# Merging the low-rank and the preparation stage of the RWKV-7 mixer, with the key products spread over other engines

## The reference, cut to what matters

```python
r, k, v = jnp.einsum('pbtd,pde->pbte', xs[:3], w_rkv)
w = -jax.nn.softplus(-(w0 + jnp.tanh(xw @ w1) @ w2)) - 0.5
a = jax.nn.sigmoid(a0 + (xa @ a1) @ a2)
g = jax.nn.sigmoid(xg @ g1) @ g2
kk = heads(k * k_k)
kk = kk / jnp.maximum(jnp.sqrt(jnp.sum(kk * kk, -1, keepdims=True)), 1e-12)
k = k * (1 + (a - 1) * k_a)
decay = jnp.exp(-jnp.exp(heads(w)))
# the scan then takes r, decay, k, v, -kk and kk * a, and
# sum(r * k * r_k) over a head weighs v in a bonus term
```

## Time and profile before

| what | value |
|---|---|
| median of three runs | 1500.87 us |
| the profiled execution | 1502.7 us |
| its span | 1501.0 us |
| mean granted TensorE clock | 0.968 of full |
| TensorE busy (matmul) | 1407.5 us, 94% |
| VectorE busy | 853.3 us, 57% |
| ScalarE busy | 679.3 us, 45% |
| GpSimd busy | 233.0 us, 16% |

### The profile page before, as it was taken

How to read it: one execution, slowest core, us unless ns; L and a number is a source line. 1 busy time by engine, 2 the same in 40 slices (tenths; PEclk the granted TensorE clock), 3 DMA queues, 4 the chain that set the end, 5 groups by cost and what they waited for, 6 DMA issues and landing times. The chain is left out here.

```text
span 1501.0 us, 18775 instructions
## 1 busy us (share of the span) xinstructions
PE 1407.5 (94%) x7494; PEld 1135.2 (76%) x7494; DVE 853.3 (57%) x1158; ACT 679.3 (45%) x992; POOL 233.0 (16%) x127
## 2 busy tenths in 40 slices
PE   6999899989999989889999998998999998999998
PEld 2685467967888877467788886887887788977887
DVE  0764685467555454546755446566545677645564
ACT  1442343136444353344643334654563657426562
POOL 0003443004000022120400000120001332500110
PEclk7899799989999999799999999999999999999999
DMA  9655457074656556635566535952542453007940
GB/s 343 206 196 160 166 200 278 1 245 122 211 180 210 180 183 204 229 112 168 169 192 200 184 137 148 198 177 83 184 162 74 156 173 107 29 29 193 226 143 29
DMA packets 159395, 247.17 MB, mean 165 GB/s; under 512 B 14086, under 2 KB 98026, under 8 KB 158796
## 3 DMA queue, kind: packets, MB, share of 16 engines
q1 hardware_dynamic: 157980, 239.60, 50.8%
q0 software_dynamic: 1328, 6.38, 1.2%
HBM read 244.85 MB, written 4.24 MB: 166 GB/s over the span
## 5 line engine op out<-in xcount | busy, mean ns | idle before, releaser
L199 DVE TENSOR_TENSOR w_lo<-w_raw,w_hi 128x2048 fp32r<-128x2048 f32 (+3 forms) x176 | 411.7, 2348 | 293.5 <-ACT w_hi L190 293.4
L211 PE MATMUL ps<-w_hi,act_hi 128*128 128x512 f32 (+4 forms) x1216 | 471.3, 388 | 13.3 <-DVE w_lo L199 4.7
L213 PE MATMUL ps<-w_hi,act_lo 128*128 128x512 f32 (+4 forms) x1216 | 461.9, 380 | 0.0
L212 PE MATMUL ps<-w_lo,act_hi 128*128 128x512 f32 (+4 forms) x1216 | 461.5, 380 | 0.0
L190 ACT CAST w_hi<-w_raw 128x2048 fp32r<-128x2048 f32 (+3 forms) x176 | 316.9, 1806 | 254.6 <-PE ps L213 209.8
L211 PEld LDWEIGHTS ps<-w_hi,act_hi 128*128 128x128 f32 x1216 | 229.9, 189 | 60.2 <-issue 14.8
L213 PEld LDWEIGHTS ps<-w_hi,act_lo 128*128 128x128 f32 x1216 | 229.5, 189 | 38.4
L212 PEld LDWEIGHTS ps<-w_lo,act_hi 128*128 128x128 f32 x1216 | 230.1, 189 | 34.5 <-issue 0.5
L320 PE MATMUL ps<-w_raw,condz 128*32 128x512 f32 x384 | 63.3, 766 | 18.7 <-DMA w_raw<-in_ada_w 14.7
L672 POOL TENSOR_TENSOR nstat<-nstat,con 128x1 f32<-128x1 f32 x8 | 5.4, 678 | 429.4 <-DVE nstat L667 429.4
L211 PE MATMUL ps<-w_hi,ffn_gh 128*128 128x512 f32 x176 | 69.1, 393 | 0.0
(11 more groups left out here) (489 smaller groups left out, 1798.2 us busy)
## 6 DMA issues: line engine op xcount, KB each, us to landing
w_raw<-in_ada_w SPq DMA_DIRECT2D x48, 1024.0 KB, 6.8
w_raw<-in_ffn_w_in SPq DMA_DIRECT2D x88, 512.0 KB, 4.8
w_raw<-in_fox_w_in SPq DMA_DIRECT2D x32, 912.0 KB, 8.7
w_raw<-in_ffn_w_out SPq DMA_DIRECT2D x20, 1024.0 KB, 5.0
w_raw<-in_rwkv_w_rkv SPq DMA_DIRECT2D x12, 1024.0 KB, 6.3
w_raw<-in_gla_w_in SPq DMA_DIRECT2D x10, 896.0 KB, 4.9
w_raw<-in_gdn_w_in SPq DMA_DIRECT2D x10, 896.0 KB, 4.9
w_raw<-in_fox_w_out SPq DMA_DIRECT2D x8, 1024.0 KB, 5.1
```

What stands on the lines that cost most here:

```text
L199: self.nc.vector.tensor_tensor(lo[:, s, 0:c["nk"], 0:c["width"]], self.raw[:, c["slot"], 0:c["nk"], 0:c["width"]], hi[:, s, 0:c["nk"], 0:c ...
L211: nc.tensor.matmul(out(t)[:, 0:w], xh[:, k, tok], hi[:, s, j, 0:w], start=start, stop=False)
L212: nc.tensor.matmul(out(t)[:, 0:w], xh[:, k, tok], lo[:, s, j, 0:w], start=False, stop=False)
L213: return nc.tensor.matmul(out(t)[:, 0:w], xl[:, k, tok], hi[:, s, j, 0:w], start=False, stop=stop)
```

## The change

`stage_rwkv_lora` and `stage_rwkv_prepare` become one stage, `stage_rwkv_low`. The product of k with `k_k`, its squares, their sums and the limit from below go to VectorE in `stage_rwkv_in`, behind the last two chunks, as do the two input mixes for `w1` and `g1`; the rows `k_k` and `k_a` are loaded there. In the new stage the down products of `a1` and `w1` alternate and write different halves of the partitions in two banks; the last 32 columns of `g1` come later, behind the cumulative sums; the gate's up products come after the sums across tiles. The scale of the rates moves into the exponentials. VectorE's work on k and GpSimd's product of a and kk go tile by tile. The bonus sums go to the start of the next stage. The new stage has three modulation items where the two old ones had four, and `stage_rwkv_mid` has ten where it had nine.

The diff, cut (the bodies of the two removed functions and the placing of buffers are left out):

```diff
...
-def stage_rwkv_in(core, m, h, dx, xs, low_w):
+def stage_rwkv_in(core, m, h, dx, xs, low_w, key):
     nc, a, ps = core.nc, core.a, core.ps
     w1, a1, g1 = low_w
+    kk, st, k_a = key
+    k_k = core.gates
...
         @block.sync
         def _(sp):
@@ -1343,8 +1349,11 @@
             sp.dma_start(g1[:, :, :], a["rwkv_g1"][0].rearrange("(k p) n -> p k n", p=P)).then_inc(sem("low_w"), 16)
             core.issue(sp, chunks[len(chunks) // 2]["g"])
             sp.dma_start(core.con[:, 2 * P:], a["consts"][:, 2 * P:]).then_inc(core.consts, 16)
+            sp.dma_start(k_k[:, :], a["rwkv_k_k"].broadcast_to([P, D])).then_inc(sem("k_k"), 16)
+            sp.dma_start(k_a[:, :], a["rwkv_k_a"].broadcast_to([P, D])).then_inc(sem("k_a"), 16)
             core.issue(sp, chunks[-1]["g"] + 1 + NRAW)
             sp.wait_ge(sem("low_w"), 48)
+            sp.wait_ge(sem("k_a"), 16)
             sp.wait_ge(core.consts, 16)
         @block.tensor
...
-            steps(lambda c: core.split_lo(dve, hi, lo, c), lambda n: None, operand, mixed)
+            def keys(n):
+                if n == 2 * per + 2:
+                    dve.wait_ge(sem("k_k"), 16)
+                    dve.wait_ge(sem("taken"), 4 * NT)
+                    nc.vector.tensor_tensor(kk[:, :, :], m.k[:, :, :], bc_out(k_k[:, :], NT), ALU.mult).then_inc(sem("kk"), 1)
+                if n == 2 * per + 3:
+                    dve.wait_ge(sem("kk"), 1)
+                    nc.vector.tensor_tensor(flat(m.lw), flat(kk), flat(kk), ALU.mult).then_inc(sem("kk"), 1)
+                    dve.wait_ge(sem("kk"), 2)
+                    nc.vector.reduce_sum(st[:, 0:32], by_head(m.lw), axis=AX_X).then_inc(sem("kk"), 1)
+                    dve.wait_ge(sem("kk"), 3)
+                    nc.vector.tensor_scalar(st[:, 32:64], st[:, 0:32], 1e-24, None, ALU.max).then_inc(sem("kk"), 1)
+            steps(lambda c: core.split_lo(dve, hi, lo, c), lambda n: None, operand, mixed, keys)
             mixed(3)
...
+            mix(core, dve, sem, 3, dx, h, decay_in)
+            mix(core, dve, sem, 5, dx, h, gate_in)
+def stage_rwkv_low(core, m, w, xs, low_w, key, at, free, items):
+    nc, a, ps = core.nc, core.a, core.ps
+    kn, st, k_a = key
+    kk, rk = w["kk"], w["rk"]
...
+    ada = Ada(core, w["ada_at"], items, 3, 2)
+    with core.stage("rwkv_low") as (block, sem):
+        @block.sync
+        def _(sp):
+            sp.dma_start(w2[0:64, :], a["rwkv_w2"][0]).then_inc(sem("w2"), 16)
+            sp.dma_start(w2[64:65, :], a["rwkv_w0"]).then_inc(sem("w2"), 16)
+            sp.dma_start(a2[0:64, :], a["rwkv_a2"][0]).then_inc(sem("a2"), 16)
+            sp.dma_start(a2[64:65, :], a["rwkv_a0"]).then_inc(sem("a2"), 16)
+            sp.dma_start(g2[:, 0, :], a["rwkv_g2"][0, 0:P]).then_inc(sem("g2"), 16)
+            sp.dma_start(g2[0:32, 1, :], a["rwkv_g2"][0, P:160]).then_inc(sem("g2"), 16)
+            sp.dma_start(w["rows"][:, 2, :], a["rwkv_r_k"].rearrange("a h j -> a (h j)").broadcast_to([P, D])).then_inc(sem("r_k"), 16)
+            core.issue_mod(sp, items)
+            sp.wait_ge(sem("r_k"), 16)
+        @block.tensor
+        def _(pe):
+            def up(u, parts):
+                if u >= 4:
+                    pe.wait_ge(sem("up_out"), u - 3)
+                c = u % 2 * COLS
+                for n, (x, down) in enumerate(parts):
+                    r = nc.tensor.matmul(ps[:, 4 + u % 4, :], x, down[:, c:c + COLS], start=(n == 0), stop=(n == len(parts) - 1))
+                r.then_inc(sem("up"), 1)
+            def cum(t):
+                for i, tri in enumerate(("cum_in", "cum_ex")):
+                    for c in range(2):
+                        r = nc.tensor.matmul(ps[:, 4 * t + 2 * i + c, :], core.c(tri), m.lw[:, t, c * COLS:c * COLS + COLS],
+                                             start=True, stop=True)
+                    r.then_inc(sem("cum"), 1)
+            for k in range(KD):
+                nc.tensor.matmul(ps[0:64, 0, 0:T], a1[:, k, :], xs[:, k, :], start=(k == 0), stop=(k == KD - 1))
+                r = nc.tensor.matmul(ps[64:P, 1, 0:T], w1[:, k, :], decay_in[:, k, :], start=(k == 0), stop=(k == KD - 1))
+            r.then_inc(sem("down"), 1)
+            for k in range(KD):
+                r = nc.tensor.matmul(ps[:, 2, 0:T], g1[:, k, 0:P], gate_in[:, k, :], start=(k == 0), stop=(k == KD - 1))
+            r.then_inc(sem("down"), 1)
+            pe.wait_ge(sem("ones"), 1)
+            pe.wait_ge(sem("low"), 2)
+            for i, (x, n) in enumerate(((w2, "w2"), (a2, "a2"))):
+                pe.wait_ge(sem(n), 32)
+                for t in range(NT):
+                    for c in range(2):
+                        up(4 * i + 2 * t + c, [(low[0:65, i, 0, t * P:t * P + P], x[0:65, :])])
+            pe.wait_ge(sem("low"), 3)
+            pe.wait_ge(sem("up_out"), 4)
+            cum(0)
+            pe.wait_ge(sem("up_out"), 8)
+            cum(1)
+            pe.wait_ge(sem("exps"), 2)
+            for k in range(KD):
+                r = nc.tensor.matmul(ps[0:32, 0, 0:T], g1[:, k, P:160], gate_in[:, k, :], start=(k == 0), stop=(k == KD - 1))
+            r.then_inc(sem("down"), 1)
+            pe.wait_ge(sem("exps"), 3)
+            for k in range(KD):
+                nc.tensor.matmul(ps[:, 1, k:k + 1], m.lw[:, 0, k * P:k * P + P], core.c("half1"), start=True, stop=False)
+                r = nc.tensor.matmul(ps[:, 1, k:k + 1], m.lw[:, 1, k * P:k * P + P], core.c("half0"), start=False, stop=True)
+            r.then_inc(sem("across"), 1)
+            ada.pe_sums(pe, sem, 0)
+            pe.wait_ge(sem("g2"), 32)
+            pe.wait_ge(sem("low"), 4)
+            pe.wait_ge(sem("exps"), 6)
+            for t in range(NT):
+                tok = slice(t * P, t * P + P)
+                for c in range(2):
+                    up(8 + 2 * t + c, [(low[:, 2, 0, tok], g2[:, 0, :]), (low[0:32, 2, 1, tok], g2[0:32, 1, :])])
+            ada.pe_turn(pe, sem, 0)
+            for n in range(1, len(items)):
+                ada.pe_sums(pe, sem, n)
+                ada.pe_turn(pe, sem, n)
+        @block.scalar
+        def _(act):
+            act.wait_ge(sem("down"), 1)
+            nc.scalar.activation(low[0:64, 0, 0, :], ps[64:P, 1, 0:T], ACT.Tanh).then_inc(sem("low"), 1)
+            nc.scalar.copy(low[0:64, 1, 0, :], ps[0:64, 0, 0:T]).then_inc(sem("low"), 1)
+            act.wait_ge(sem("down"), 2)
+            nc.scalar.activation(low[:, 2, 0, :], ps[:, 2, 0:T], ACT.Sigmoid).then_inc(sem("low"), 1)
+            for u in range(8):
+                i, t, c = u // 4, u // 2 % 2, u % 2
+                act.wait_ge(sem("up"), u + 1)
+                nc.scalar.activation((m.lw, m.a)[i][:, t, c * COLS:c * COLS + COLS], ps[:, 4 + u % 4, :], ACT.Sigmoid).then_inc(sem("up_out"), 1)
+            for t in range(NT):
+                act.wait_ge(sem("cum"), 2 * t + 2)
+                c_in = ps[:, 4 * t:4 * t + 2, :].rearrange("p a b -> p (a b)")
+                c_ex = ps[:, 4 * t + 2:4 * t + 4, :].rearrange("p a b -> p (a b)")
+                nc.scalar.activation(ep[:, t, :], c_in, ACT.Exp, scale=-shrink).then_inc(sem("exps"), 1)
+                nc.scalar.activation(en[:, t, :], c_in, ACT.Exp, scale=shrink).then_inc(sem("exps"), 1)
+                nc.scalar.activation(ex[:, t, :], c_ex, ACT.Exp, scale=-shrink).then_inc(sem("exps"), 1)
+            act.wait_ge(sem("across"), 1)
+            nc.scalar.activation(w["across"][:, :], ps[:, 1, 0:KD], ACT.Exp, scale=-shrink).then_inc(sem("across_e"), 1)
+            act.wait_ge(sem("down"), 3)
+            nc.scalar.activation(low[0:32, 2, 1, :], ps[0:32, 0, 0:T], ACT.Sigmoid).then_inc(sem("low"), 1)
+            ada.act_part(act, sem, 0)
+            for u in range(8, 12):
+                t, c = u // 2 % 2, u % 2
+                act.wait_ge(sem("up"), u + 1)
+                nc.scalar.copy(m.g[:, t, c * COLS:c * COLS + COLS], ps[:, 4 + u % 4, :]).then_inc(sem("up_out"), 1)
+            for n in range(1, len(items)):
+                ada.act_part(act, sem, n)
+        @block.gpsimd
+        def _(pool):
+            nc.gpsimd.tensor_tensor(st[:, 32:64], st[:, 32:64], core.c("mhalf")[:, 0:32], ALU.pow).then_inc(sem("rn"), 1)
+            pool.wait_ge(sem("kn"), 1)
+            for t in range(NT):
+                pool.wait_ge(sem("up_out"), 6 + 2 * t)
+                pool.wait_ge(sem("less"), t + 1)
+                nc.gpsimd.tensor_tensor(A[:, t, :], A[:, t, :], kn[:, t, :], ALU.mult).then_inc(sem("kka"), 1)
+        @block.vector
+        def _(dve):
+            link = Link(dve, sem("dve"))
+            v = nc.vector
+            v.memset(low[64:65, 0:2, 0, :], 1.0).then_inc(sem("ones"), 1)
+            dve.wait_ge(sem("rn"), 1)
+            v.tensor_tensor(by_head(kn), by_head(kn), bc_in(st[:, 32:64], 64), ALU.mult).then_inc(sem("kn"), 1)
+            dve.wait_ge(sem("kn"), 1)
+            for t in range(NT):
+                dve.wait_ge(sem("up_out"), 6 + 2 * t)
```

(30 more changed lines are left out.)

148 lines of the change are left out of this document (16 added, 132 removed).

## The result

The changed kernel takes 1507.38 us (median of 13 runs, 1499.02 to 1518.56), the kernel before beside it 1503.3 (13 runs, 1496.52 to 1508.19): **ratio 1.0039, 95% interval 1.0022 to 1.0057**, some 3 to 9 us slower. The forecast was 1502.8 and "no difference". The measured median lies inside the range of 1495 to 1509, but a small loss clear of noise was measured where none was forecast. The 1502.8 was reckoned from 1500.87, the median of three runs; 13 runs of the kernel before have 1503.3, so 2.4 of the 4.6 us between forecast and median are the starting value. As a change, +1.9 us was forecast, and +4.1 by the medians or +5.9 by the ratio was measured. The profiled execution took 1506.51 us, its span is 1504.8.

What follows compares the result with a forecast made beforehand. TensorE's queue was taken to bound the two merged stages, 36.3 and 21.5 of 1501 us. Merged stage −2.3, mid's start −1.4 and mid's end +5.6 sum to +1.9 us: 1502.8 on the median, range 1495 to 1509.

Steps and rivals of the forecast that it cites:

- sign of being wrong: Mid's tail: the prediction is wrong if it grows by less than 3 or more than 8 us.
- End of mid: Mid's tail: the tenth item goes where nothing covers it and its chunks land late, +5.6 us (ends +3.0 and +7.7).
- outer end: Mid's tail: turns at the lower clock, 1.87 us each instead of 1.0, making the tail +7.7 us.
- End of the input stage: Input stage: with its added work VectorE ends it at 122.1 instead of ScalarE at 119.74, +2.35 us.
- Down products: Merged stage: a1 and w1 overlap in alternate column halves, 3.65 us for the pair; −4.1 us together, −0.45 without overlap.
- Gate's up products: Merged stage: following one-column products, they run 4 us at half clock, +2.0 us (ends 0 and +4).
- Table loads: Merged stage, ScalarE: two loads of 1.28 us, the second done before TensorE asks; costs nothing.
- Items and the wait for chunk 5: Merged stage's end: TensorE waits from 169.7 to 171.3 for a late-issued chunk, then half an item at lower clock.
- Start of mid: Mid's start: the small rel_bias load arrives 5.1 us after the start instead of 6.5, −1.4 us (ends −2.2 and 0).
- bunched items: Slower rival: no chunk issued for 29 us in the merged stage, price at both tails; +8.7 us, 1509.6, chance 0.13.

Runs made afterwards that it cites:

- Experiment 1: Kernel before with only one modulation item moved from the preparation stage to mid (ten there): 1505.86 us, ratio 1.0019.
- experiment 4: Changed kernel plus four useless 512-column products on TensorE behind the recurrence, to keep the tail's clock up: 1506.24 us, ratio 1.0030.
- experiment 9: Changed kernel with all down products of a1 ahead of those of w1 instead of in turn: 1511.41 us, ratio 1.0063.
- experiment 3: Changed kernel with the input mix for g1 back in the merged stage, under the down products of a1 and w1: 1503.93 us, ratio 1.0013.
- experiment 10: Changed kernel with the product of a and the normalized keys on VectorE instead of GpSimd: 1509.63 us, ratio 1.0036.
- experiment 6: Changed kernel with eight items in mid's loop instead of seven, one fewer in the tail: 1501.48 us, ratio 0.9986.
- experiment 5: Changed kernel with the merged stage's first item early, behind the down products: 1509.0 us, ratio 1.0040.
- experiment 7: Changed kernel with gate mix back in the merged stage, first item early and eight items in mid's loop: 1502.93 us, ratio 0.9984.
- Experiment 12: Changed kernel with gate mix back, four items spread through the merged stage, seven in mid's loop, two in its tail: 1494.05 us, ratio 0.9932.
- experiment 2: Changed kernel with the item's move undone, four items in the merged stage and nine in mid: 1502.87 us, ratio 1.0000.
- experiment 8: Changed kernel with gate mix back, four items spread through the merged stage, nine in mid, eight of them in its loop: 1494.33 us, ratio 0.9938.

## Why the prediction was wrong

The sum was +1.9 us; the profile says +5.24. The tail grew by more than the 8 us that the prediction had named as a sign of being wrong. Term by term the account is off by −0.3 (idle time), +1.3 (merged stage), −1.7 (start of mid and recurrence), +3.3 (tail) and +0.8 (next head), together the 3.3 that were missing.

- **End of mid, the step that failed: +5.6 forecast, +8.87 measured**, outside the ends of +3.0 and +7.7. Up to the end of the second item's products the tail is as before. I had the last chunk land 13.1 us behind the first instruction of the tail (319.4 against 306.26) and half an item and turns at full clock behind it. It landed 1.2 us later (issued 7.4 us behind that instruction, 0.2 later than reckoned, and 6.9 us on its way instead of 6.0), and after TensorE had waited 0.82 and 2.54 us the clock was low: half an item 1.93 instead of about 1, and 16 turns 3.57 instead of 1.95. I had taken the low turns as an outer end, with no wait that brings them about; a wait and the clock behind it belong into one term. Experiment 1 shows that this term has nothing to do with the rest of the change (+8.31 there), experiment 4 that the two halves are coupled.
- **Next head, missing: +0.80.** The transposes of the next stage follow on the tail and begin at its clock. Experiment 1 has nearly the same tail and a next head of 5.60 us, as before, so the 0.80 is not shown to belong to the change.
- **End of the input stage: +2.35 forecast, +2.04 measured.** VectorE ended 20.9 us after it began chunk 10 (99.15 to 120.08), as worked out (21.3). The product with `k_k` took 2.28, not 4.32: no GpSimd instruction stood beside it. In the merged stage, where one did, the same kind of product took 3.25, and 1.23 once it was gone (experiment 10). The rule of the Trainium skill that the prediction drew on ("SBUF — State Buffer", section "Who interferes with whom": two SBUF inputs on VectorE contend with GpSimd's reads, as an exclusive lock) agrees with both.
- **Down products: −4.1 forecast, about −2.4 measured.** The overlap is real (experiment 9, and 3.7 us for the pair in experiment 3). What I did not follow is what my own +2.35 does: TensorE stands idle for 3.46 us instead of 1.42, the clock falls to 0.50 during the pair (so in seven of the eight profiles with this idle time, see the last section), and it takes 5.3 instead of 3.65. That I costed the idle time as its length alone is the second failed step.
- **Gate's up products: +2.0 forecast, +1.2 measured** (9.60 us). They stood at the low clock only at first: 0.70 on the mean of 150 to 154 us, 0.87 in the next 4. In experiments 4 and 6, with the same code, they took 8.47 us: the term can be nothing.
- **Table loads: nothing, and so it was.** ScalarE ahead of them in the changed kernel:

```profile
150.43 0.18 ACT L1536 ACTIVATE across<-ps 128x8 f32<-128x8 f32 x1 [4.37 <-PE ps L1502]
150.63 1.28 ACT L1538 ACT_TABLE_LOAD   x1
151.92 0.37 ACT L1538 ACTIVATE low<-ps 32x256 f32<-32x256 f32 x1
```

From the end of the exponential to the sigmoid it is 1.31 us, and TensorE asked at 152.68. The Trainium skill ("ScalarE: Activation LUTs", section "What ACT_TABLE_LOAD costs") has some 2.66 us with a drain; this row does not agree, no drain is to be seen.

- **Items and the wait for chunk 5: 1.6 forecast, 1.72 measured**, half an item at the lower clock as forecast, and its turn at the lower clock too (1.87), which was not. In experiments 4 and 6 the same wait (1.54 and 1.79) was followed by both at full clock (1.06 and 1.05). In all the merged stage with the idle time ahead ended 1.35 us earlier than the two old ones, not 2.3.
- **Start of mid: −1.4 forecast, −3.08 measured to the end of the recurrence: −3.52 in mid's head, +0.44 in the loop.** TensorE had no wait for `rel_bias` left and the first masked copy came at 6.9 us, when VectorE was free, as worked out; and by 182 us the clock had recovered, where it was low into the same stretch before. This gain comes from the item that left: experiment 1 has 5.0 us of it, and the changed kernel 1.5 less, since VectorE now sums the bonus there first. It is not firm: in the five experiments with three items in the merged stage that still wait 1.6 to 1.9 us for `rel_bias` (3 to 7), the head takes 27.4 or 27.5. Stretches as above, first the kernel before, then the changed kernel:

```profile
182.00:200.00 18.00, 15.75 (x102) 10.76 (x104) 8.24 (x12) 6.57 (x13) 12.95 (x6) 0.81 0.65 222
```

```profile
182.00:200.00 18.00, 15.94 (x118) 10.97 (x118) 13.46 (x18) 7.64 (x15) 11.51 (x8) 1.00 0.55 177
```

Of the rivals, that of the bunched items had much of the mechanism (late chunks, a price at both tails). Its 1509.6 us is nearer to the median than the forecast only by the starting value: as changes, +1.9 and +8.7 stand on either side of the +4.1 to +5.9 measured. I gave it 0.13 and let it decide from a landing of 7.5 us. The median landing of the tail's chunks was 6.9, below that. So the tail's price came without long landings: nothing was issued in time, and the clock was low behind the waits there. Its gain at mid's start was not lost either.

**What stays open.** What makes the clock fall after one idle time and not after another of the same length (below). And what spreading the items is worth by itself. Experiment 12 lies some 6 us below the sum of edits 2 and 3, but experiment 8 does not lie below the sum of edits 2, 3 and 6 (1.0% against 1.2% under the changed kernel), with a noise of 3 us and more on each ratio. The profiles show the waits gone, but the loop varies by up to 5 us between profiles of the same code.

## What to carry to other kernels

Filler work pays only where something covers it and its data are at hand: moving one item into an uncovered tail cost 8 us there, more than it gave back elsewhere, and moving it back took away the changed kernel's loss (experiments 1 and 2). What an item gives back has to be looked for in the next stage too, and it is capped where another engine then ends the stage. Before stages are merged to save products, ask what TensorE does at the seam, since an engine that is made to wait 2 us longer may then run at half its clock for some us more, and spread the filler between other products, so that each use frees a buffer and starts a load early. When an edit seems to shorten a stage, look at the next one and at a profile in which that stage's code is unchanged before counting the gain: here unchanged code ran 3.3 us shorter in one profile than in another, and the head of the next stage took 2.8 of it back at the low clock.
